# Eight more 128x512 matmuls per head in the SSM diagonal stage of a two-layer hybrid encoder

## What is computed

```python
def segsum_exp(a):
    cs = jnp.cumsum(a, axis=-1)
    diff = cs[..., :, None] - cs[..., None, :]
    t = a.shape[-1]
    mask = jnp.tril(jnp.ones((t, t), dtype=bool))
    return jnp.exp(jnp.where(mask, diff, -jnp.inf))
...
    Lmat = segsum_exp(a)
    y_diag = jnp.einsum('bclgn,bcsgn,bgrcls,bcsgrp->bclgrp', Cc, Bc, Lmat, xd)
```

## Time and profile before

| | |
|---|---|
| median of 3 runs | 3207.79 us (3207.36 to 3213.49) |
| the profiled execution | 3205.44 us, of which the span from first to last instruction 3203.7 us |
| PE busy | 3024.3 us, 94% of the span |
| DVE, ACT, POOL busy | 54%, 32%, 8% |
| mean granted TensorE clock over the span | 0.946 of full speed |
| PE on the chain that ended last | 76% of the span |

### The profile page before, as it was taken

The page is one execution under the profiler, slowest core; times in us unless marked ns, Lnnn a source line. Parts: engine busy times, 40 slices in busy tenths (PEclk is TensorE's granted clock), DMA queues, the critical chain, the costliest instruction groups (busy, mean ns, idle before and its releaser), DMA issues.

```text
span 3203.7 us, 33957 instructions
## 1 busy us (share of the span) xinstructions
PE 3024.3 (94%) x13850; PEld 2401.2 (75%) x13850; DVE 1726.0 (54%) x2004; ACT 1015.7 (32%) x1480; POOL 249.7 (8%) x171
## 2 busy tenths in 40 slices
PE   6899998998799999999998999999798999999997
PEld 5667776766667878888885788888676878888886
DVE  7777865564456343333348767776737433333335
ACT  2213315411233111212125555665614212121122
POOL 2420002254100000000000000000000000000000
PEclk7999996599889999999998999999998999999998
DMA  5455474013311111111113011111121111111111
GB/s 198 150 164 174 147 235 157 10 40 118 125 46 46 47 46 53 46 46 52 46 54 109 21 39 46 52 39 53 60 92 40 53 46 47 53 46 46 52 46 59
DMA packets 270484, 240.19 MB, mean 75 GB/s; under 512 B 6861, under 2 KB 249006, under 8 KB 270318
## 3 DMA queue, kind: packets, MB, share of 16 engines
q1 hardware_dynamic: 257334, 185.61, 18.9%
q0 software_dynamic: 11984, 48.61, 4.0%
q10 hardware_dynamic: 1040, 4.19, 0.3%
HBM read 209.36 MB, written 36.90 MB: 77 GB/s over the span
## 4 chain that ended last, share of the span: by engine, by line
PE 76%; DVE 4%; ACT 2%; DMA 1%; issue 1%; POOL 1%; POOLq 0%; ACTq 0%; DVEq 0%
PE psum_gemm L218 10%; PE psum_gemm L222 10%; PE psum_gemm L219 10%; PE psum_gemm L1781 7%; PE psum_misc L218 6%; PE psum_misc L219 6%; PE psum_misc L222 6%; PE psum_gemm L333 3%; PE psum_misc L1845 2%; PE psum_gemm L1866 2%; PE psum_gemm L1854 2%; PE psum_misc L1250 2%; PE psum_gemm L1263 1%; PE psum_gemm L1259 1%; PE psum_gemm L1867 1%
## 5 line engine op out<-in xcount | busy, mean ns | idle before, releaser
L218 PE MATMUL psum_gemm<-h_hi,w_hi 128*128 128x512 f32 x2000 | 793.3, 397 | 29.3 <-POOL h_lo L407 19.5
L219 PE MATMUL psum_gemm<-h_lo,w_hi 128*128 128x512 f32 x2000 | 781.8, 391 | 0.0
L222 PE MATMUL psum_gemm<-h_hi,w_lo 128*128 128x512 f32 x2000 | 618.6, 391 | 0.0
L218 PEld LDWEIGHTS psum_gemm<-h_hi,w_hi 128*128 128x128 f32 x2000 | 377.5, 189 | 132.0 <-issue 40.1
L219 PEld LDWEIGHTS psum_gemm<-h_lo,w_hi 128*128 128x128 f32 x2000 | 377.8, 189 | 78.9 <-issue 2.9
L222 PEld LDWEIGHTS psum_gemm<-h_hi,w_lo 128*128 128x128 f32 x2000 | 377.0, 189 | 79.0
L1566 ACT ACTIVATE w_hi<-w_raw 128x1024 fp32r<-128x1024 f32 x130 | 137.3, 1057 | 562.9 <-PE psum_misc L222 349.2
L218 PE MATMUL psum_misc<-ffn_act_hi,w_hi 128*128 128x512 f32 x704 | 276.0, 392 | 4.7 <-DVE ffn_act_lo L1674 4.7
L219 PE MATMUL psum_misc<-ffn_act_lo,w_hi 128*128 128x512 f32 x704 | 275.2, 391 | 0.0
L200 ACT ACTIVATE w_hi<-w_raw 128x1024 fp32r<-128x1024 f32 x79 | 83.2, 1055 | 510.1 <-PE psum_gemm L222 386.2
L1686 DVE TENSOR_TENSOR mix_out<-mix_out,psum_misc 128x1024 f32<-128x1024 f32 x80 | 97.7, 1221 | 231.3 <-PE psum_misc L222 231.3
(11 more groups left out here) (315 smaller groups left out, 4714.4 us busy)
## 6 DMA issues: line engine op xcount, KB each, us to landing
w_raw<-in_f_w_up SPq DMA_DIRECT2D x88, 512.0 KB, 3.8
ada_w<-in_w_ada SPq DMA_DIRECT2D x40, 1024.0 KB, 5.3
w_raw<-in_f_w_down SPq DMA_DIRECT2D x44, 512.0 KB, 3.4
w_raw<-in_e_w_in SPq DMA_DIRECT2D x29, 512.0 KB, 6.4
w_raw<-in_o_w_qkv SPq DMA_DIRECT2D x24, 512.0 KB, 3.8
ada_w_first<-in_w_ada SPq DMA_DIRECT2D x4, 2048.0 KB, 18.7
w_raw<-in_e_w_out SPq DMA_DIRECT2D x16, 512.0 KB, 4.1
skew_scratch<-bias_scratch POOLq DMA_DIRECT2D x1, 7680.0 KB, 48.9
```

The lines of the kernel that those rows point to most:

```text
L218: pe.matmul(o, wh, rh[:, k, c], start=(k == 0), stop=False)
L219: pe.matmul(o, wh, rl[:, k, c], start=False, stop=False)
L222: last = pe.matmul(o, wl, rh[:, k, c], start=False, stop=(k == nk - 1))
```

## The change

In front of the two selector matmuls of every fill stand four more matmuls, each with the identity as weights and one direction's mask repeated four times as the moving operand, 128x512, two into each bank of `pG[:, d]`. They start and stop their own accumulation, and the selector matmul that follows starts a new one on the same bank, so nothing reads what they write. They stand behind the fill's wait. 4 x 2 directions x 16 heads = 128 instructions are added (and as many weight loads); nothing is removed and nothing else moves.

```diff
@@ -1255,6 +1255,9 @@
                     hd = 16 * d + h
                     if h >= 1:
                         pe.wait_ge(s_exp, 2 * h - 1 + d)
+                    for n in range(4):
+                        pe.matmul(pG[:, d, n % 2 * HALF:(n % 2 + 1) * HALF], identR[:],
+                                  maskR[:, d:d + 1].to_broadcast([P, 4, P]), start=True, stop=True)
                     for n in range(2):
                         pe.matmul(pG[:, d, n * HALF:(n + 1) * HALF], selR[:, hd:hd + 1].to_broadcast([64, P]),
                                   T2[:, n * HALF:(n + 1) * HALF], start=True, stop=False)
```

## The result

The changed kernel runs in 3186.3 us (median of 4 runs, 3184.66 to 3192.01) against 3208.58 us before on the same chips (4 runs): the ratio is 0.9933, interval 0.9921 to 0.9946. Forecast were 3188 us, with 3181 to 3200 as the range.

What follows compares the result with a forecast made beforehand. PE was taken to bound the kernel, at half clock throughout the diagonal stage. Terms +2.4, -19.7, -4.1, 0 and +1.5 sum to -19.9 us, from 3207.8 to 3188 us; range 3181 to 3200.

Steps and rivals of the forecast that it cites:

- The clock rises and holds: Diagonal stage: dense added streams raise PE's clock from 0.50 to 1.00 in the first head or two, and it holds.
- second rival: Diagonal stage: the clock does not rise and each added matmul costs 0.43 us; 3261 us, slower; chance 0.10.
- y: PE's 16 float32 instructions of 64 columns per head: 1.79 us at the high clock, against 3.31 before.
- Heads 0 to 3, +2.4: Diagonal stage's first heads, fills only: +1.9 us in head 0, +0.5 in heads 1 to 3.
- Twelve heads, -19.7: The heads where y alternates with fills: 6.27 us a head instead of 7.91, so -19.7 us.
- Tail, -4.1: From last fill to last y: 9.5 us instead of 13.6, the fourth y waiting for its weight tile.
- DVE with POOL, +1.5: Diagonal stage: DVE and POOL, getting in each other's way, now and then bind for a moment, +1.5 us.
- my bound of 6.0: Least time per head that DVE with POOL allow: 5.28 us plus 0.75 for the evacuation of y.
- The next stage, 0: Stage after the diagonal one: starts again at 0.50, 3.9 us at the low clock; between -1.9 and +1.7, taken as 0.

Runs made afterwards that it cites:

- 64-row run: Four added matmuls per fill, but with the 64-row selector as weights and cumulative sums as moving operand, against the kernel before: 3264.88 us, ratio 1.0172.
- padded kernel: No added matmuls; selector and cumulative sums padded with zeros from 64 to 128 rows, against the kernel before: 3173.88 us, ratio 0.9889.

## Why the prediction was right

Between the two profiled executions (3205.44 and 3185.8 us) lie 19.6 us. By the prediction's own terms, against the chain and the timeline of both:

- **The clock rises and holds.** It did, and in the first two heads as forecast: at 525.3 us, in the third fill, which is head 1's first. The reason given, few holes in the stream of columns, is not enough: the 64-row run has the same holes as the change and never rose. What made the difference stood in the second rival as something that "no row shows", that rows or data matter. Whether holes matter too no run shows by itself. The forecast that the clock would hold leaned on attention's stage with its 64-row weights; here it did not hold on fills of the old kind, as the run with four in the first heads shows. With one matmul fewer the rise is a matter of chance, and with two fewer there is none. That four were enough is therefore luck in part, and the forecast was surer of this step than its rows allowed.
- **y.** The prediction reads the weight loads as about half of y. Its own row says otherwise: in the last y's PEld is busy for 13.35 of 13.50 us. The half served the argument on the clock, not the sum; y came out at 1.73 us against 1.79.
- **Heads 0 to 3, +2.4.** Measured from the first matmul to the first y on the chain: 538.03 - 514.61 = 23.4 us, before 532.51 - 514.20 = 18.3: +5.1. This is the term that was mis-sized. The sum let head 0 pay for most of one fill at the low clock; the run had more than two and a half. Where the clock rose at 519.9 us over the same instructions (the run with four in heads 0 to 3), the first y came 535.61 - 515.08 = 20.5 us behind the first matmul, against 532.31 - 514.20 = 18.1 before by the same timeline: the +2.4 of the forecast. So the term hangs on chance, and the prediction had no range for it.
- **Twelve heads, -19.7.** 613.06 - 538.03 = 75.0 us, before 627.39 - 532.51 = 94.9: -19.9. The 6.27 us a head were 6.26.
- **Tail, -4.1.** 622.80 - 613.06 = 9.7 us, before 13.6: -3.9, with the wait for the last tile and the fall of the clock in it.
- **DVE with POOL, +1.5.** Nothing: PE was busy without a gap. In the padded kernel DVE with POOL binds at 5.3 us; my bound of 6.0 had added the evacuation's 0.75 to the 5.28 of the first heads, and it doesn't add: with the evacuation in front of it, the add starts 0.68 us behind POOL's multiply (565.57 against 564.89) instead of 0.04, and takes 2.31 us instead of 2.95. The Trainium skill's "SBUF — State Buffer" (SBUF: two separate sides) says why it may be so: only an instruction of DVE with two inputs in SBUF, or in one of its two-port modes, contends with POOL. The trace agrees: the evacuation, with one input in PSUM, kept 0.74 us beside POOL, and the add took 2.31.
- **The next stage, 0.** It starts at 625.7 and is at speed at 631.1 us, 5.4 us at the low clock against 3.9; some 0.8 us of work lost.

The stage's terms and its start, 0.4 us later, make -18.2 before rounding (622.80 against 640.98 us), and the rest of the program is 1.5 us shorter in this execution, lost microseconds at the next stage's start included. What that rest is I didn't follow; the runs of the kernel before differ by 6 us among themselves. Two errors, +2.7 in the first heads and -1.5 for POOL, and this rest of -1.5 nearly cancelled: that the total came within 0.3 us of the -19.9 is luck. A slip in the range: its upper end, summed from the terms named (a head of 6.8, tail 10.3, start +1.7), is -11, not -10.

On the Trainium skill's rule, "TensorE: Matmul & The Clock Gate" (Part 1: The HAM clock gate): activity releases the throttle. The runs agree with it only if activity is not the profile's busy share: with two added matmuls PE was busy for 130.00 of 130.00 us at 0.50, and in the padded kernel for 55.20 of 71.40 at 1.00. Nor is it the streams alone, as the prediction read it: the 64-row run streams as densely as the change and stayed at 0.50.

## What to carry to other kernels

Look for stretches where PE is busy and its granted clock is half; there the question is not how to give PE less to do but what its instructions look like. Here weights that use 64 of 128 rows mattered; weight loads that stand alone may matter as well, which no run here separates. Pad the useful matmuls to full rows first (that gave 35 us and needed no filler). Unused matmuls are a second choice: here four per fill gained 22 us, three were a gamble, and two were pure cost. Test such a change by many executions and look at their spread, since at the edge the same kernel ran in 3182.6 and in 3215.0 us; the change itself was run four times only.

## What was unexpected

- Mostly zeros in 128 rows (identity and mask, or padding) went with a rising clock, and 64-row streams of real data did not raise it in 166 us of unbroken work. So it is not that real values are needed; 64-row streams of zeros were not tried.
- With the added matmuls in the first four heads only, the clock stayed up for 20 us behind the last of them (534 to 554 us) before it fell.
- A change of row count costs PE 0.2 us even at the full clock: 5.5 against 6.26 us a head with the same matmuls.
